# Cached pages on 16 partitions with eight rows each, in place of 32 partitions with four rows

## The chip, the cores and the metric

The kernel runs on one core of a Trainium2 chip. The metric is the device time of one execution, in microseconds; lower is better. Everything is float32.

## The reference, cut to what matters

One inference step of a two-layer decoder, for a prompt of 512 tokens and for 8 sequences of 8 new tokens each, which share all weights. Layer 0 has attention (differential attention over a paged cache, and a dilated window attention), layer 1 a convolution, and each layer ends in a mixture of 32 experts. The change lies in layer 0, in the attention of the 8 sequences over their cached pages:

```python
k_all = concatenate([cache_k_diff[i][page_table].reshape(n_dec, past, H_DIFF, 2 * HEAD_DIM), kd_new], axis=1)
v_all = concatenate([cache_v_diff[i][page_table].reshape(n_dec, past, H_DIFF, DV_DIFF), va], axis=1)
oa = diff_core(q1, q2, k_all[..., :HEAD_DIM], k_all[..., HEAD_DIM:], v_all, lam, pos_s, k_pos_s)
```

Each sequence has 2,048 cached positions in 16 pages of 128 rows. A row is 512 floats (2 KB), so a page is 256 KB, and a sequence's page keys and page values are 4 MB each. All new tokens may see all cached positions, so in which order the cached positions lie on the chip is free, as long as keys and values have the same one. Beside the pages each sequence has a window cache, of which 1,280 rows of keys and as many of values are read (2.5 MB each).

## The kernel before, in words

**Stages.** The projections of layer 0 run until about 200 us from the span's start. From 200 to 540 us comes the attention: the 64 items of the prompt (`prompt_*`) are interleaved with the 8 sequences b = 0 to 7. The output projection, the experts of layer 0 (both from 541 to 1,130 us), layer 1 and its experts follow; the change touches none of them.

**Buffers.** `Kd` and `Vd` hold the page keys and page values of one sequence, [128 partitions, 16, 512]; `Wkv` holds the window's keys, and after them the window's values. None of them is doubled: the next sequence's data can come only when the products of the last one have read the buffer.

**Loads.** `pages_in` (L553) issues one DMA for each page. Page j goes to partitions j % 4, j % 4 + 4, and so on, which is 32 partitions, and on each of them to four neighbouring places of the middle axis, with 8 KB in one piece. `window_far` (L559, three DMAs) and `window_near` (L564, one) load the window over all 128 partitions. The keys are issued by SyncE (SP), the values by GpSimd (POOL). An engine issues in the order of its code, so the order for sequence b is:

```python
sp.wait_ge(sd_mm, b)
pages_in(sp, pages[0:8], 0, ck, Kd, kd_in)
sp.wait_ge(pv_w, b)
window_far(sp, b, wk, kw_in)
window_near(sp, b, wk, kw_in)
pages_in(sp, pages[8:], 8, ck, Kd, kd_in)
```

POOL does the same with the values (L2553 to L2562): it waits for `pv_d` (the page value products of b - 1 are done), issues pages 0 to 7, waits for `sw_mm` (the window scores of b are done), issues the window and then pages 8 to 15. Below, K-first and K-second are the first and last eight pages of keys, V-first and V-second those of values.

**Use.** VectorE turns the page keys in place in 32x32 blocks, four of the 16 places at a time: `turn_pages(b, k)` (L1278) waits for the semaphore `kd_in[k]`, which the pages 4k to 4k + 3 raise. In the loop of VectorE (from L1498) the order is: k = 2 and 3 of sequence b after the window's maximum, and at the end of the round k = 0 and 1 of sequence b + 1 and then the two turns of its window keys. TensorE then computes the window scores (`window_scores`, L2048, semaphore `sw_mm`), the page scores (`page_scores`, L2063, `sd_mm`; they need all four turns), the window value products (`window_products`, L2110, `pv_w`, needs the window values), and the page value products (`page_products`, L2128, `pv_d`, needs all 16 pages of values). A round, here, is the time from the end of one sequence's page scores to the end of the next one's.

`page_numbers` (L548) reads the page table. `load_x` (L2508) is used below as a measure: after the attention it reads the prompt rows of x into 128 partitions and then the 64 sample rows into partitions 0 to 63.

Of the kernel before, what the change touches and what calls it, by code (L numbers as in the profile page):

```python
# [126 lines left out]
def build(nc, x_prompt, x_sample, ck, cv, wk, wv, st_rows, st_cols, ptab, w_in, w_out, w_pw1, w_pw2,  # L127
# [9 lines left out]
    def sem(name):  # L137
        return ctx.enter_context(nc.semaphore(name))
# [152 lines left out]
    kd_in, vd_in = [sem(f"kd_in{i}") for i in range(4)], [sem("vd_in")] * 4  # L291
# [13 lines left out]
    X_TILE = [16, 48, 16, 16, 16]  # L305
# [246 lines left out]
    def pages_in(eng, pages, first, src, dst, arrived):  # L552

        for j, page in enumerate(pages, first):
            held = dst[j % 4::4, j // 4 * 4:j // 4 * 4 + 4, :].rearrange("p n c -> p (n c)")
            rows_of = src[bass.ds(page, 1)].rearrange("a (p e) c -> (a p) (e c)", e=4)
            eng.dma_start(held, rows_of).then_inc(arrived[j // 4], 16)  # L557

    def window_far(eng, b, src, arrived):  # L559
# [16 lines left out]
    def _(sp):  # L576
# [36 lines left out]
        for i in range(4, 8):  # L613
            copy_window(i)
        sp.wait_ge(z_mm, Z_MM[1, "p4_1"])
        pages_in(sp, pages, 0, ck, Kd, kd_in)
        for b in range(1, NB):
            pages = page_numbers(sp, b)
# [6 lines that stand above are left out]
# [577 lines left out]
    def _(dve):  # L1202
# [75 lines left out]
        def turn_pages(b, k):  # L1278
            if not 0 <= b < NB:
                return  # L1280
            keys = Kd[:, 4 * k:4 * k + 4, :].rearrange("p n c -> p (n c)")
            dve.wait_ge(kd_in[k], X_TILE[k] + 64 * (b + 1))
            V.transpose(keys, keys).then_inc(kd_turned, 1)  # L1283

        link(V.memset(B(12288, 1024), 0.0))
# [43 lines left out]
        for w in range(3):  # L1329
# [33 lines left out]
            if w == 2:  # L1363
                turn_pages(0, 0)
# [4 lines left out]
            if w == 2:  # L1369
                turn_pages(0, 1)  # L1370
# [4 lines left out]
            if w == 2:  # L1375
                turn_pages(0, 2)
# [1376 lines left out]
```

## Time and profile before

| What | Value |
|---|---|
| Median of 3 runs | 1948.61 us (1948.54 to 1952.93) |
| The profiled execution's own time | 1950.49 us |
| Its span | 1948.5 us |
| PE busy | 1624.7 us, 83% |
| DVE busy | 695.3 us, 36% |
| DMA, mean rate over the span | 338 GB/s |
| Attention stage, end of the first to end of the eighth page scores | 239 to 520 us |

The span is the time between the first and the last instruction of the one execution that was profiled. Its own time is 2 us more than the span, and 1.9 us above the median. "DMA share" is the mean busy share of the 16 DMA engines, "GB/s" what they moved; a share can read a few per cent above 1, since a packet is counted where it starts.

### The profile page before, as it was taken

The numbers are of one execution on the slowest core, as the hardware profiler recorded it, in microseconds if no ns is written. First come the engines' busy times: TensorE is split into PE (matmuls) and PEld (weight loads), VectorE is DVE, ScalarE is ACT, GpSimd is POOL, SyncE is SP. The second block draws the span as 40 slices with busy tenths as digits, with TensorE's granted clock in tenths as the row PEclk, the third lists the DMA queues.
The fourth block names the chain that finished last, engine by engine and source line by source line (L and its number), as shares of the span: only waits on it lengthen the run. The fifth ranks groups of instructions, "written<-read, shape, count | busy, mean of one in ns | idle before, by whom it ended". The sixth has DMA issues, their size and how long they took to land.

```text
span 1948.5 us, 32623 instructions
## 1 busy us (share of the span) xinstructions
PE 1624.7 (83%) x12772; PEld 773.9 (40%) x12772; DVE 695.3 (36%) x1351; ACT 331.3 (17%) x769; POOL 213.5 (11%) x356
## 2 busy tenths in 40 slices
PE   7999788888898888878877879998968877877784
PEld 3444355555545322222222347764532222323231
DVE  4446478866514300000000159984260000000005
ACT  3100254444302000000000020013120000000001
POOL 1000222322200100000000030000021000000000
PEclk9999799978898899998999989999979989999998
DMA  9995489988853899999999999923269999999995
GB/s 347 346 357 194 178 322 358 362 323 333 349 221 136 332 428 426 409 429 427 428 427 428 415 289 322 324 99 162 80 255 426 428 416 418 427 428 427 428 426 206
DMA packets 83829, 659.20 MB, mean 338 GB/s; under 512 B 15307, under 2 KB 15436, under 8 KB 45418
## 3 DMA queue, kind: packets, MB, share of 16 engines
q1 hardware_dynamic: 58906, 569.86, 73.6%
q0 software_dynamic: 24800, 87.65, 12.0%
q8 instruction: 82, 1.34, 0.3%
q14 instruction: 41, 0.34, 0.0%
HBM read 643.18 MB, written 96.53 MB: 380 GB/s over the span
## 4 chain that ended last, share of the span: by engine, by line
PE 51%; DMA 34%; DVE 8%; issue 3%; ACT 2%; SPq 1%; POOLq 0%; DVEq 0%; POOL 0%; ACTq 0%
DMA ring<-in 30%; PE ps L2294 14%; PE ps L2249 7%; PE ps L2457 6%; PE ps L1874 6%; PE ps L1838 4%; PE ps L2063 2%; DMA ring<-y_rows 2%; PE ps L2478 2%; DVE ring L1283 2%; PE ps L2048 1%; PE ps L2314 1%; PE ps L2003 1%; DMA out<-x 1%; DVE ring L1276 1%
## 5 line engine op out<-in xcount | busy, mean ns | idle before, releaser
L2294 PE MATMUL ps<-ring,big 128*32 128x512 f32 (+1 forms) x2688 | 468.6, 645 | 134.0 <-DMA ring<-in 128.1
L2294 PEld LDWEIGHTS ps<-ring,big 128*32 128x32 f32 (+1 forms) x2688 | 146.9, 130 | 451.2 <-issue 381.2
L1555 DVE TENSOR_TENSOR big<-big,ps 128x512 f32<-128x512 f32 x32 | 22.0, 687 | 822.5 <-PE ps L2294 777.4
L2314 PE MATMUL ps<-ring,big 128*32 128x512 f32 (+1 forms) x928 | 215.7, 606 | 20.2 <-ACT big L797 12.3
L797 ACT ACTIVATE big<-ps 128x512 f32<-128x512 f32 (+6 forms) x166 | 84.2, 516 | 819.4 <-PE ps L1838 517.4
L2249 PE MATMUL ps<-ring,big 128*128 128x512 f32 (+1 forms) x288 | 122.7, 608 | 5.7 <-ACT big L1191 4.8
L2457 PE MATMUL ps<-act_t,ring 128*128 128x288 f32 x512 | 124.4, 406 | 0.0
L2314 PE MATMUL ps<-act_t,big 128*32 128x512 f32 (+1 forms) x416 | 99.0, 594 | 15.5 <-ACT big L797 10.5
L2457 PEld LDWEIGHTS ps<-act_t,ring 128*128 128x128 f32 x512 | 97.2, 190 | 26.8
L1779 DVE SCALAR_TENSOR_TENSOR big<-big,par 128x512 f32<-128x512 f32 x240 | 103.8, 503 | 0.0
L1874 PE MATMUL ps<-ring,act_t 128*128 128x512 f32 x208 | 94.8, 604 | 6.1 <-DMA ring<-in 4.1
L2314 PEld LDWEIGHTS ps<-ring,big 128*32 128x32 f32 (+1 forms) x928 | 63.6, 125 | 89.0 <-issue 89.0
L2602 POOL COPY sti<-sti 128x1 int32 (+1 forms) x30 | 5.5, 182 | 759.4 <-ACT big L797 759.4
L1838 PE MATMUL ps<-cst,big 128*128 128x128 f32 (+2 forms) x472 | 69.5, 296 | 21.9 <-DMA big<-h_rows,sti 8.8
L557 POOL DMA_DIRECT2D ring<-in x128 | 66.5, 524 | 193.8 <-PE ps L2128 179.9
L1838 PEld LDWEIGHTS ps<-cst,big 128*128 128x128 f32 (+2 forms) x472 | 59.9, 192 | 55.3 <-issue 30.1
L2249 PEld LDWEIGHTS ps<-ring,big 128*128 128x128 f32 (+1 forms) x288 | 51.1, 188 | 71.3 <-issue 68.6
L1283 DVE STREAM_TRANSPOSE ring<-ring 128x2048 f32<-128x2048 f32 x32 | 72.3, 2290 | 0.6 <-DMA ring<-in 0.6
L1109 ACT ACTIVATE big<-ps 128x512 f32<-128x512 f32 x32 | 19.1, 597 | 300.8 <-PE ps L2294 286.4
L1838 PE MATMUL ps<-cst,x 128*128 128x128 f32 (+1 forms) x312 | 54.8, 290 | 14.1 <-ACT x L797 9.4
L1874 PEld LDWEIGHTS ps<-ring,act_t 128*128 128x128 f32 x208 | 38.8, 193 | 50.9 <-issue 44.3
L2314 PEld LDWEIGHTS ps<-act_t,big 128*32 128x32 f32 (+1 forms) x416 | 28.6, 118 | 74.2 <-issue 74.2
(322 smaller groups left out, 1771.2 us busy)
## 6 DMA issues: line engine op xcount, KB each, us to landing
ring<-in SPq DMA_DIRECT2D x180, 2048.0 KB, 18.5
out<-in SPq DMA_DIRECT2D x16, 4080.0 KB
ring<-in SPq DMA_DIRECT2D x128, 256.0 KB, 7.0
ring<-in POOLq DMA_DIRECT2D x128, 256.0 KB, 5.8
act_t<-in SPq DMA_DIRECT2D x16, 2048.0 KB
ring<-in SPq DMA_DIRECT2D x28, 1024.0 KB, 10.1
ring<-in SPq DMA_DIRECT2D x24, 512.0 KB, 6.2
ring<-in POOLq DMA_DIRECT2D x24, 512.0 KB, 4.9
```

Of the source, the lines that this page charges most:

```text
L557: eng.dma_start(held, rows_of).then_inc(arrived[j // 4], 16)
L797: return A_(o, i, ACT.Copy)
L1283: V.transpose(keys, keys).then_inc(kd_turned, 1)
L1779: S(V.scalar_tensor_tensor(o, i, wdw[:, ch, j:j + 1], o, ALU.mult, ALU.add))
L1838: return nc.tensor.transpose(o, i, ident[0:n, 0:n])
L1874: ins = mm(ps[:, bank, :], lhs[:, k, :], rhs[:, k, :], start=(k == 0), stop=(k == 3))
L2063: ins = mm(ps[32 * c:32 * c + 16, g, :].rearrange("p (n k) -> p n k", n=16), Qrep[p, d, 16 * c:16 * c + 16], Kd[p, :, c * P + 32 * d:c * P ...
L2249: ins = mm(ps[unit_rows(t, j), i % 4, :], lhs(k, t), slot(slots_[n], 8)[:, k, :], start=(k == 0), stop=(k == KC - 1))
L2294: ins = mm(ps[half, i, :], XgT[:, par_, k, half], slot(eslots(w)[i], 8)[:, k, :], start=(k == 0), stop=(k == KC - 1))
L2314: ins = mm(ps[half, 5 + h, :], hbT[:, k, half], down_weights(w, odd)[:, k, h * 512:(h + 1) * 512], start=(k == 0), stop=(k == 3))
L2457: ins = mm(ps[:, 4 * (ch % 2) + 2 * i + h, 0:HALF], slot(first + i, 8)[:, k, (ch % 4) * P:(ch % 4 + 1) * P], act_t[:, k, h * HALF:(h + 1) ...
L2478: ins = mm(ps[32 * a:32 * a + 32, 4 + g, :], diag[p, 32 * a + j, :], taken, start=(j == 0), stop=(j == CK))
```

## The change: what it does

Page j now goes to partitions j % 8, j % 8 + 8, and so on, which is 16 partitions, and on each to eight neighbouring places, with 16 KB in one piece. Pages 0 to 7 together fill places 0 to 7 of the middle axis on all 128 partitions, pages 8 to 15 places 8 to 15. A turn of four places now needs eight pages, so the waits ahead of the turns k = 0 and k = 2 are for both semaphores of their half, and the turns k = 1 and k = 3 have no wait of their own.

```diff
     def pages_in(eng, pages, first, src, dst, arrived):
 
         for j, page in enumerate(pages, first):
-            held = dst[j % 4::4, j // 4 * 4:j // 4 * 4 + 4, :].rearrange("p n c -> p (n c)")
-            rows_of = src[bass.ds(page, 1)].rearrange("a (p e) c -> (a p) (e c)", e=4)
+            held = dst[j % 8::8, j // 8 * 8:j // 8 * 8 + 8, :].rearrange("p n c -> p (n c)")
+            rows_of = src[bass.ds(page, 1)].rearrange("a (p e) c -> (a p) (e c)", e=8)
             eng.dma_start(held, rows_of).then_inc(arrived[j // 4], 16)
...
             keys = Kd[:, 4 * k:4 * k + 4, :].rearrange("p n c -> p (n c)")
-            dve.wait_ge(kd_in[k], X_TILE[k] + 64 * (b + 1))
+            if k % 2 == 0:
+                for i in (k, k + 1):
+                    dve.wait_ge(kd_in[i], X_TILE[i] + 64 * (b + 1))
             V.transpose(keys, keys).then_inc(kd_turned, 1)
```

No instruction is added, removed or moved on any engine; on each engine they stand in the same order as before. What differs is the shape of the 256 page DMAs (128 on SP, 128 on POOL) and the waits of the turns.

## Rows read from the trace of the kernel before

**Rows 1.** The page, part 2: 40 equal slices of 48.7 us.
```profile
PEclk9999799978898899998999989999979989999998
DMA  9995489988853899999999999923269999999995
GB/s 347 346 357 194 178 322 358 362 323 333 349 221 136 332 428 426 409 429 427 428 427 428 415 289 322 324 99 162 80 255 426 428 416 418 427 428 427 428 426 206
```
**Rows 2.** Windows, one for each round: busy us, TensorE clock, DMA share, GB/s.
```profile
239.00:278.00 39.00, 35.15 (x679) 22.36 (x665) 31.18 (x42) 19.57 (x56) 10.57 (x20) 1.00 0.90 335
278.00:321.00 43.00, 36.55 (x694) 23.18 (x694) 33.23 (x57) 19.20 (x58) 10.36 (x20) 0.96 0.85 318
321.00:358.00 37.00, 33.62 (x668) 21.86 (x669) 29.43 (x44) 19.18 (x58) 10.37 (x20) 1.00 0.96 362
358.00:398.00 40.00, 32.73 (x661) 20.19 (x659) 30.34 (x54) 17.51 (x57) 10.37 (x20) 1.00 0.96 367
398.00:442.00 44.00, 38.88 (x651) 24.34 (x652) 28.02 (x44) 17.76 (x58) 10.36 (x20) 0.77 0.83 314
442.00:481.00 39.00, 32.31 (x643) 19.27 (x642) 28.59 (x55) 16.26 (x57) 9.85 (x19) 0.87 0.87 330
481.00:520.00 39.00, 32.27 (x634) 19.10 (x633) 26.41 (x44) 16.63 (x60) 10.89 (x21) 0.82 0.95 374
```
**Rows 3.** The chain that ended last, 355 to 520 us: start, us, what.
```profile
353.33 4.48 PE ps L2063 x128
...
396.83 1.07 PE ps L2063 x15
...
405.06 3.78 PE ps L2110 x80
...
412.50 1.00 PE ps L2128 x32
...
417.86 1.00 PE ps L2128 x32
...
488.37 7.48 DMA ring<-in
```
**Rows 4.** Timeline of SP, the issues of the keys.
```profile
146.58 10.82 SPq L557 DMA_DIRECT2D ring<-in  x16
...
239.59 5.06 SPq L557 DMA_DIRECT2D ring<-in  x8
...
357.98 5.14 SPq L557 DMA_DIRECT2D ring<-in  x8
364.36 2.48 SPq L562 DMA_DIRECT2D ring<-in  x3
366.88 0.59 SPq L566 DMA_DIRECT2D ring<-in  x1
367.66 6.13 SPq L557 DMA_DIRECT2D ring<-in  x8
398.14 6.20 SPq L557 DMA_DIRECT2D ring<-in  x8
```
**Rows 5.** Timeline of POOL, the issues of the values.
```profile
377.42 4.55 POOL L557 DMA_DIRECT2D ring<-in  x8 [23.74 <-PE ps L2128]
384.55 1.60 POOL L562 DMA_DIRECT2D ring<-in  x3 [2.58 <-PE ps L2048]
386.11 0.58 POOL L566 DMA_DIRECT2D ring<-in  x1
386.62 2.75 POOL L557 DMA_DIRECT2D ring<-in  x5
389.71 1.67 POOL L557 DMA_DIRECT2D ring<-in  x3 [0.34 <-issue]
```
**Rows 6.** Timeline of DVE, the turns of keys (L1283 pages, L1276 window).
```profile
175.96 2.30 DVE L1283 STREAM_TRANSPOSE ring<-ring 128x2048 f32<-128x2048 f32 x1
...
386.07 4.50 DVE L1283 STREAM_TRANSPOSE ring<-ring 128x2048 f32<-128x2048 f32 x2
...
411.46 4.50 DVE L1283 STREAM_TRANSPOSE ring<-ring 128x2048 f32<-128x2048 f32 x2
416.14 5.57 DVE L1276 STREAM_TRANSPOSE ring<-ring 128x3072 f32<-128x3072 f32 x2 [0.18 <-DMA ring<-in]
```
**Rows 7.** Windows: us, TensorE clock, DMA share, GB/s.
```profile
350.00:358.00 8.00, 1.00 1.03 422
...
547.00:548.00 1.00, 1.00 1.03 422
549.00:549.50 0.50, 1.00 0.83 164
549.50:550.00 0.50, 1.00 0.49 115
```
**Rows 8.** DMA landings: all page loads of L557, then DMAs issued 541 to 552 us.
```profile
DMA to landing us min/median/max: 2.9/6.4/17.5
...
x<-in POOLq DMA_DIRECT2D x1, 2048.0 KB, 8.7
x<-in POOLq DMA_DIRECT2D x1, 256.0 KB, 9.2
```

## The prediction

> **What bounds the kernel now.** I read the slices of the page first [rows 1]. Slices 5 to 10 are the attention: DMA is at eight or nine tenths of its time there, yet it moves 322 to 362 GB/s, where the expert stages (slices 14 to 21, 30 to 38) move about 428. So the queues are nearly full, but not saturated. The windows by round say the same more finely [rows 2]: seven rounds in 281 us, 40.0 us each, with PE busy for 34.5 us of a round and DVE for 29.6. The chain of waits [rows 3] runs through the engines in these rounds; a DMA of any length (7.48 us) stands in it only once, in the last round. The kernel is thus bound in this stage by the engines' own order of work, with the DMAs close behind.
>
> How close, I work out for one round. The page scores of one sequence end at 353.33 + 4.48 = 357.81 us, those of the next at 396.83 + 1.07 = 397.90 [rows 3]. Four batches of eight pages (2.10 MB each) and two windows (2.62 MB each) move in a round, 13.6 MB. In 350 to 358 us, when the value window and V-second are in flight, the rate is 422 GB/s at a share of 1.03 [rows 7]. At that rate a page takes 0.62 us, a batch 5.0 and a window 6.2, and a round has 4 x 5.0 + 2 x 6.2 = 32.4 us of DMA work in 40.0. The slack is 7.6 us, no more.
>
> **The change part by part.** *Issues.* SP needs 5.14 to 6.20 us for eight page DMAs and POOL 4.55 us [rows 4, 5]. Their number stays. The bounds are nothing and half (if the time goes by the rows of the DMA); I take nothing, because POOL issues a window DMA in 1.60 / 3 = 0.53 us and a page DMA in 4.55 / 8 = 0.57 [rows 5], although the window's has many more rows.
>
> *The waits of the turns.* The turns k = 0 and k = 1 stand back to back (4.50 us for both) [rows 6], so it is the first that now waits for pages 4 to 7 as well, 2.3 us earlier than they were wanted. K-first is issued from 398.14 to 404.34 [rows 4] and turned from 411.46 [rows 6], 7.1 us after its last issue; a page lands in 6.4 us (median, 2.9 at best) [rows 8]. At the rate of before this wait costs 0 to 1 us and I take 0. K-second: issued by 373.79, turned at 386.07, hidden by 12 us [rows 4, 6].
>
> *The transfers.* Here the change is decided. The pieces are 16 KB in place of 8 KB, which can help a little: the expert loads move 428 GB/s against 422 [rows 1, 7], 1.4%, 0.07 us in a batch. But a page now reaches only 16 partitions. The trace has one load that reaches a part of the partitions: the sample rows of x, into partitions 0 to 63, behind the prompt rows of x into all 128. While the latter run, the rate is 422 GB/s at a share of 1.03, which is 410 per full share. In the half microsecond when little but the 64-partition load is left, it is 164 at 0.83, which is 198, and in the next 115 at 0.49, 235 [rows 7]. The engines are busy and move half. (The small load also lands last though it is an eighth of the other: 9.2 us against 8.7 [rows 8].) So there are ways into the on-chip memory which DMA engines have to share if a transfer leaves the other ways out; and 32 partitions in steps of four do not have this trouble, they run at 422 [rows 7]. Whether steps of eight have it, no row shows. The bounds: full rate, 5.0 us a batch (4.9 with the longer pieces), and half rate, 9.9 us a batch of 2.10 MB at 211 GB/s. I take the half rate, since the 64-partition load is the nearest row in kind: 16 partitions cannot reach more ways than there are partitions, and the 32 of before may have needed all of theirs.
>
> The Trainium skill states the map ("SBUF — State Buffer", the section on the DMA port swizzle): bits 2 to 4 and bit 6 of the partition number pick one of 16 ports, so four neighbours share a port with the four that lie 32 further. By that rule j % 4 + 4m reaches all 16 ports, and j % 8 + 8m, in which bit 2 is fixed, only 8; pages 0 to 3 of a batch all go to the same 8 and pages 4 to 7 to the other 8. The row of the 64-partition load agrees with its statement that 0 to 63 reach 8 ports. By it a batch takes 9.9 us, and the sum is the one below; without the fixed bit it would be 5.0 us and the sum zero.
>
> *What half rate does to a round.* The DMA work becomes 4 x 9.9 + 2 x 6.2 = 52.0 us, against a round of 40.0: the cover of 7.6 us is gone and the DMAs are the bound. Not all of it is serial. When a page of the one queue and a page of the other go to different halves, both run, and 9.9 us of work counts 5. Follow the values: V-first is issued at 377.42, the window at 384.55, V-second at 386.62 [rows 5]. With 2 us until data flow they alone take 26.0 us, until 405.4 at the earliest, and later by some 3 us for the K-second batch that is still under way (K window and K-second issued from 364.36 [rows 4]: 364.4 + 2 + 6.2 + 9.9 = 382.5). Before, they needed 16.2 us and were done before 398. Now V-second still runs for about 10 us when K-first of the next sequence is issued at 398.14. K-first then takes 9.9 us if the two always lie in different halves, 19.8 if they never do; between these ends I take 15.5. It lands at 398.1 + 2.2 + 15.5 = 415.8, where the turns stood ready at 411.46 [rows 6]: a wait of 4.3 us. Behind it on the same queue the window of the keys (6.2 us) is free to start only then: 422.0 + 0.5, where its turn, shifted by the 4.3, stood at 420.4: 2 more. V-second itself is late by little: its products start at 412.50 [rows 3] and it ends near 411 to 418; I put 1 to 2 us, of which 1 lies beside the other waits. And all of DVE's work behind the turns (window maxima, page maxima, softmax of the prompt items) and PE's scores shift with them, nothing covers it. That makes about 7.5 us. The clock adds some: where PE has paused, the granted clock falls to the lower level, and the round at 0.77 took 44 us against 37 to 40 for those at 1.00 [rows 2]. With one pause of 6 us in each round I put 1.5 us for it, since part of a slower PE is waited out beside the DMAs anyway. A round comes to 49 us (+9), between +7 (halves always apart: 40.0 + 7) and +12 (52.0, no overlap at all).
>
> *The sum.* The rounds are not alike. The first has an idle queue ahead (K-first at 239.59 [rows 4], its V-second issued long before): +1. Six rounds at +9: +54. After the last page scores the last V-second (issued by 513.6) ends near 525, where its products begin at about 528: +1 with the output weights that run beside it. The page keys of the first sequence are issued from 146.58, with 16 x 0.6 us more work, and turned from 175.96 on [rows 4, 6]: hidden. Nothing outside the stage changes. 1 + 54 + 1 = **+56 us**. Against the profiled execution, 1950.5 + 56 = 2006.5; it stood 1.9 us above the median, so by the median the result is 1948.6 + 56 = 2004.6, about **2005 us**, +2.9%.
>
> **The rivals.** *The halves get out of step.* Two engines that share a way need not both be on the same half: if one gets ahead by four pages, it writes the second half while the other writes the first, and both run at full rate. For it: the rounds of before reach 422 although nothing tells the engines to alternate [rows 7]. Against it: a lead of four pages is 64 KB, a whole batch must then wait for the laggard, and batches of eight end often. A batch would take 7.5 us, the round 4 x 7.5 + 12.4 = 42.4 us of work with gaps of 2 to 4: about +3 a round, 1948.6 + 20 = 1969 us.
>
> *The ways are runs of eight partitions.* Steps of eight then reach each of them, batches stay at 5.0 us, and only the wait of the pair is left, 0 to 1 us in 7 rounds: 1945 to 1952, no change. The rows don't exclude it; the 64-partition row fits it as well.
>
> *Coarser pieces pay.* The other side: half the pieces, and issues that get cheaper with them. SP's eight page DMAs would take 5.1 - 1.5 us, and K-second, the window and V would land 1 us earlier; where turns follow landings at once (the window's, 0.18 us of idle [rows 6], and the 7.48 us in the chain [rows 3]), a round gains up to 1 us. 1948.6 - 7 = 1941 us. It decides if the DMA, not the engines' order, sets the window's turn in most rounds; the chain shows it in one.
>
> *It goes worse.* If one shared way also holds up what stands behind it in both queues, windows too, the work is 60 us a round: +18, 2055 us.
>
> **How the numbers follow.** What a measurement of this kernel can tell from no change is about 0.3%, 6 us. Half rate as forecast (1985 to 2035) 0.65; out of step (1957 to 1985) 0.13; worse (above 2035) 0.07; no change 0.09; faster 0.06. Slower takes the first three, 0.85; same 0.09; faster 0.06. The range reaches from 1960, which takes in nearly all of the second case, to 2040: some 0.2 is left out.
>
> **What would show it.** In the profile after: page batches in flight alone at about 211 GB/s with the DMA share near 1 (step 1); rounds of 47 to 52 us, the DMA share above 0.95 in each (step 2); turns of L1283's line idle before them for a DMA, 3 to 8 us in six of seven rounds, and the window's 1 to 3 (step 3); the stages from the output projection on as before, only later. The forecast is wrong if batches run at 400 GB/s or more, or if the share is full at half the rate and the rounds are still 40 us.

## The result, and the profile after

The change makes the kernel slower: 2068.63 us median of 4 runs (2059.91 to 2081.10), against 1948.57 us, the median of 4 runs of the kernel before beside it. The ratio is 1.062, with a 95% interval of 1.058 to 1.066. The direction was forecast; the size was not: +120 us, where +56 was forecast and 2040 us was the upper end of the range. The profiled execution took 2081.1 us with a span of 2079.0, 12 us above the median, so the sums below are for that execution: 2079.0 - 1948.5 = +130.5 us.

The slices of the page after, as [rows 1] for before (a slice is now 52.0 us):

```profile
PEclk9999889876876979999999998999998999999897
DMA  9994799988996449999999999993228999999995
GB/s 352 340 358 145 195 246 254 253 229 218 251 230 202 183 184 404 426 429 410 427 427 428 428 424 298 325 332 126 85 109 345 428 427 413 427 429 427 427 426 214
```

In the attention (slices 5 to 11) the DMA engines are busy for eight or nine tenths of the time, as before, but they move 218 to 254 GB/s in place of 322 to 362. The expert stages are untouched at 428.

The windows by round, as [rows 2]; they begin and end where the page scores of a sequence end. The columns are length, busy time of PE, PEld, DVE, ACT and POOL, the clock, the DMA share and GB/s:

```profile
244.00:297.00 53.00, 39.17 (x693) 23.06 (x680) 32.13 (x43) 19.59 (x56) 9.95 (x20) 0.87 0.99 253
297.00:350.00 53.00, 39.30 (x685) 24.35 (x678) 32.82 (x54) 19.17 (x57) 9.92 (x20) 0.87 1.00 256
350.00:405.00 55.00, 38.40 (x677) 23.63 (x669) 30.05 (x43) 19.36 (x58) 9.92 (x20) 0.84 0.99 248
405.00:462.00 57.00, 39.96 (x663) 23.96 (x661) 30.84 (x54) 17.80 (x57) 9.92 (x20) 0.76 0.89 228
462.00:526.00 64.00, 42.70 (x656) 24.48 (x653) 28.51 (x44) 17.69 (x59) 9.92 (x20) 0.73 0.88 221
526.00:581.00 55.00, 35.01 (x641) 20.33 (x639) 28.71 (x54) 16.38 (x57) 7.99 (x16) 0.78 0.98 245
581.00:637.00 56.00, 34.60 (x644) 20.83 (x631) 26.23 (x43) 16.40 (x58) 11.86 (x24) 0.73 1.00 248
```

Seven rounds took 393.0 us, 56.1 each against 40.0. DVE has the same 30 us of work in a round, PE 38 for 34.5, part of that because its granted clock is lower (0.73 to 0.87 here; 0.77 to 1.00 in the seven rounds of [rows 2]).

The chain that ended last, in the same stage, as [rows 3]. Before, a DMA of any length stood in it once; now one stands in each of the seven rounds (the first and the last, 11.86 and 24.83 us, are left out here and end at a turn of the window keys):

```profile
314.19 24.94 DMA ring<-in
...
366.61 27.50 DMA ring<-in
...
422.68 27.41 DMA ring<-in
...
481.13 34.62 DMA ring<-in
...
542.73 26.64 DMA ring<-in
```

All five of these end where the turns k = 2 and 3 begin: the chain waits for K-second, the last load in the queue of the keys. One round of these turns (L1285 pages, L1276 window), with the idle time ahead of each in brackets:

```profile
368.64 4.50 DVE L1285 STREAM_TRANSPOSE ring<-ring 128x2048 f32<-128x2048 f32 x2 [7.39 <-DMA ring<-in]
373.88 3.38 DVE L1276 STREAM_TRANSPOSE ring<-ring 128x3072 f32<-128x3072 f32 x1 [0.74 <-DMA ring<-in]
379.91 2.31 DVE L1276 STREAM_TRANSPOSE ring<-ring 128x2048 f32<-128x2048 f32 x1 [2.65 <-DMA ring<-in]
394.21 4.50 DVE L1285 STREAM_TRANSPOSE ring<-ring 128x2048 f32<-128x2048 f32 x2 [5.26 <-DMA ring<-in]
```

Over all seven rounds K-first is waited for 49.1 us, the window keys 19.3 and K-second 27.2, which is 7.0, 2.8 and 3.9 us a round.

Who waits, in sum: the turns of the page keys (as [rows 6], where nothing or 0.18 us stood ahead of a turn) and the value products. From the costliest groups; the last columns are idle time and its releaser:

```profile
L1285 DVE STREAM_TRANSPOSE ring<-ring 128x2048 f32<-128x2048 f32 x32 | 72.3, 2292 | 76.3 <-DMA ring<-in 76.3
...
L2130 PE MATMUL ps<-ring,act_t 128*16 128x128 f32 x1024 | 46.6, 336 | 38.7 <-DMA ring<-in 35.6
```

The same turns cost the same 72.3 us as before; the 76.3 us of idle time before them was 0.6. The two longest rounds, the fourth and the fifth, are also those in which the DMA engines are not full (0.89 and 0.88). In the fourth, K-second lands at 450.09 us (422.68 + 27.41 in the chain), although the DMAs stand nearly still before that:

```profile
436.00:440.00 4.00, 0.90 0.17 47
```

A share of 0.17 is two to three engines of 16, and the packets that they move are those of the key queue. They are behind the others, and the wait is for them. Why they are behind was not looked into.

And windows in which little but page loads is in flight (as [rows 7]; in 355 to 360 us mostly K-first, in 442 to 449 V-first):

```profile
355.00:360.00 5.00, 4.78 (x101) 3.45 (x102) 3.04 (x8) 3.96 (x11) 0.00 (x0) 1.00 1.05 243
...
442.00:449.00 7.00, 5.75 (x168) 3.71 (x146) 5.37 (x15) 2.66 (x9) 5.18 (x11) 1.00 1.04 225
```

That is 231 and 216 GB/s per full share, where the loads of before gave 410 [rows 7], and the forecast took 211.

### The profile page after: what moved, and what is told of

It reads as the page before. It is cut to its first block, busy times and chain, and to the rows that moved or that the text cites. A ratio compares the mean times of both kernels' runs of the same rounds, so it can differ in the third digit from the quotient of the medians.

```text
span 2079.0 us, 32638 instructions
## 1 busy us (share of the span) xinstructions
PE 1666.6 (80%) x12772; PEld 790.6 (38%) x12772; DVE 698.3 (34%) x1351; ACT 332.3 (16%) x769; POOL 210.2 (10%) x356
## 4 chain that ended last, share of the span: by engine, by line
PE 45%; DMA 42%; DVE 5%; issue 3%; SPq 3%; ACT 1%; POOLq 1%; POOL 0%; DVEq 0%; ACTq 0%
DMA ring<-in 39%; PE ps L2296 13%; PE ps L2251 6%; PE ps L2459 6%; PE ps L1876 6%; PE ps L1840 3%; PE ps L2065 2%; DMA ring<-y_rows 2%; PE ps L2480 2%; PE ps L2316 1%; SPq L557 1%; DMA out<-x 1%; PE ps L2112 1%; PE ps L2335 1%; PE ps L2223 1%
## 5 line engine op out<-in xcount | busy, mean ns | idle before, releaser
L2316 PE MATMUL ps<-ring,big 128*32 128x512 f32 (+1 forms) x928 | 215.7, 606 | 17.8 <-ACT big L797 12.3
L1285 DVE STREAM_TRANSPOSE ring<-ring 128x2048 f32<-128x2048 f32 x32 | 72.3, 2292 | 76.3 <-DMA ring<-in 76.3
L2316 PEld LDWEIGHTS ps<-ring,big 128*32 128x32 f32 (+1 forms) x928 | 63.7, 125 | 86.5 <-issue 86.5
L557 POOL DMA_DIRECT2D ring<-in x128 | 62.4, 492 | 287.0 <-PE ps L2130 257.8
L2130 PE MATMUL ps<-ring,act_t 128*16 128x128 f32 x1024 | 46.6, 336 | 38.7 <-DMA ring<-in 35.6
L2065 PE MATMUL ps<-ring 32*16 32x512 f32 x1024 | 50.3, 801 | 29.2 <-DVE ring L1285 25.3
L1840 PE MATMUL ps<-cst,x 128*128 128x128 f32 (+1 forms) x312 | 54.9, 290 | 13.6 <-ACT x L797 9.2
```

Of the source, the lines that this page charges most:

```text
L1840: return nc.tensor.transpose(o, i, ident[0:n, 0:n])
L2065: ins = mm(ps[32 * c:32 * c + 16, g, :].rearrange("p (n k) -> p n k", n=16), Qrep[p, d, 16 * c:16 * c + 16], Kd[p, :, c * P + 32 * d:c * P ...
L2130: ins = mm(ps[32 * c:32 * c + 16, 7, P:2 * P], PT_d[:, n, 16 * c:16 * c + 16], Vd[:, n, c * P:(c + 1) * P], start=(n == 0), stop=False)
L2316: ins = mm(ps[half, 5 + h, :], hbT[:, k, half], down_weights(w, odd)[:, k, h * 512:(h + 1) * 512], start=(k == 0), stop=(k == 3))
```

## The experiments

The question was in two parts: is it the partitions that a page reaches, and why is the loss twice what that was priced at? For all kernels below I also give the window from the end of the first to the end of the eighth page scores. Its DMA share times the length of a round is what I call the **engine time** of a round: how long a DMA engine was held in it, in the mean of the 16. A **packet** is what one engine moves in one go, here one piece on one partition; the trace has the time that each took. In the expert loads a packet of 16 KB takes 0.61 us, and the shortest of 8 KB in the attention take 0.31. In the change those of the pages (16 KB) take 1.21 us in the median.

The rounds come from the one profiled execution of each kernel. Executions of one kernel differ by up to some 20 us, and in e11 by 43 us, so a difference of one or two us between rounds says little.

**e1: the waits alone.** The layout of before, with the pair waits of the change.

```diff
-            dve.wait_ge(kd_in[k], X_TILE[k] + 64 * (b + 1))
+            if k % 2 == 0:
+                for i in (k, k + 1):
+                    dve.wait_ge(kd_in[i], X_TILE[i] + 64 * (b + 1))
```

> The layout of before with the change's waits alone: the turns k = 0 and 2 wait for all eight pages of their half. Theory H (a page on partitions in steps of eight has only half of the ways into the on-chip memory): the waits are nearly free, 0 to 1 us a round, ratio to before 1.000 to 1.003. Theory W (the wait for twice the pages is what holds VectorE and all behind it): most of the +120 us stays, ratio above 1.03.

Measured: ratio 1.002 (1.000 to 1.004), rounds of 39.8 us. The waits are free, as forecast; theory W falls.

**e2: 32 partitions, but half of the ways.** Everything as before but the choice of the 32 partitions.

```diff
-            held = dst[j % 4::4, j // 4 * 4:j // 4 * 4 + 4, :].rearrange("p n c -> p (n c)")
+            lo = j % 2 + 64 * (j % 4 // 2)
+            held = dst[lo:lo + 63:2, j // 4 * 4:j // 4 * 4 + 4, :].rearrange("p n c -> p (n c)")
```

> Pages on 32 partitions with 8 KB pieces and the waits of before, but in steps of two, inside partitions 0 to 63 (pages 0, 1 of each four) or 64 to 127 (pages 2, 3). Number of partitions, size and number of pieces and the waits are all as before; only which partitions is changed. Theory H: page batches at about half rate again, the 8 KB packets take about twice their 309 ns, rounds of 50 to 57 us, ratio 1.04 to 1.07. Theory L (fewer, longer pieces or fewer partitions are what is slow): as before, ratio 1.00, rounds of 40 us.

Measured: 1.051 (1.047 to 1.055), rounds of 54.0 us. The number of partitions, of pieces, the size of a piece and the waits are those of before, and most of the change's loss is there. The 8 KB packets (a fifth of them the window's) take 0.57 us in the median, where those of before take 0.31. The rows are read from the same places in the same order as before, so it is not the source either. Theory L falls for that part.

**e3: the change in pieces of 8 KB.**

```diff
-            held = dst[j % 8::8, j // 8 * 8:j // 8 * 8 + 8, :].rearrange("p n c -> p (n c)")
-            rows_of = src[bass.ds(page, 1)].rearrange("a (p e) c -> (a p) (e c)", e=8)
+            held = dst[j % 8::8].rearrange("p (h q r) c -> p q h (r c)", h=2, q=2)[:, j // 8]
+            rows_of = src[bass.ds(page, 1)].rearrange("a (p h e) c -> (a p) h (e c)", h=2, e=4)
...
-            keys = Kd[:, 4 * k:4 * k + 4, :].rearrange("p n c -> p (n c)")
+            g = (0, 2, 1, 3)[k]
+            keys = Kd[:, 4 * g:4 * g + 4, :].rearrange("p n c -> p (n c)")
```

> The change's 16 partitions in steps of eight, but each partition's eight rows in two pieces of 8 KB that lie 16 KB apart on chip (places 0 to 3 and 8 to 11, or 4 to 7 and 12 to 15). Theory H: no better than the change, ratio 1.05 to 1.07. Theory L in the form that the 16 KB piece is slow: back to before, ratio 1.00 to 1.01.

Measured: 1.055 (1.052 to 1.058), rounds of 54.9 us, 0.60 us for a packet of 8 KB. The length of the piece is not what is slow.

**e4: neighbours in the queue in different halves.** The change, with a batch issued in another order.

```diff
-        for j, page in enumerate(pages, first):
+        for j, page in sorted(enumerate(pages, first), key=lambda jp: (jp[0] % 4, jp[0])):
```

> The change, but each batch issues its pages in the order 0, 4, 1, 5, 2, 6, 3, 7, so that neighbours in a queue go to different halves of the ways. Theory H with engines that keep in step: two engines that share a way still meet on it, ratio 1.05 to 1.07. Theory H with engines that get one page out of step (as seems to happen over 8 KB pieces before): batches near 5 to 7 us in place of 9, ratio 1.00 to 1.03. Theory L: no effect, ratio 1.06.

Measured: 1.040 (1.035 to 1.045), rounds of 50.1 us. The same bytes on the same partitions, and a third of the loss is gone: it matters which pages are in flight together. A packet takes 1.07 us, still far from 0.61: the order gives back some of the time, and not the full rate that the theory with a ratio of 1.00 to 1.03 needs.

**e5 and e6: keys alone, values alone.** `pages_in` takes w = 8 or 4 by the semaphores it is given; e5 has the pair waits too.

```diff
-            held = dst[j % 4::4, j // 4 * 4:j // 4 * 4 + 4, :].rearrange("p n c -> p (n c)")
-            rows_of = src[bass.ds(page, 1)].rearrange("a (p e) c -> (a p) (e c)", e=4)
+            w = 8 if arrived is kd_in else 4
+            held = dst[j % w::w, j // w * w:j // w * w + w, :].rearrange("p n c -> p (n c)")
+            rows_of = src[bass.ds(page, 1)].rearrange("a (p e) c -> (a p) (e c)", e=w)
```

> Only the page keys lie on 16 partitions in steps of eight (with the change's waits), the values on 32 in steps of four as before; the positions of keys and values then differ, so the attention over the pages is not the reference's. Theory S (slack: a round of 40.0 us has 32.4 us of DMA work, each half-rate batch adds 4.9 us, and only what goes past the round costs): 42.2 us of work, rounds of 41 to 44, ratio 1.01 to 1.02. Theory A (each slow batch costs its own length, however much slack there is): half of the change's loss, ratio 1.03.

> Only the page values lie on 16 partitions in steps of eight, the keys as before with the waits of before; the attention over the pages is not the reference's. Theory S: 42.2 us of work, ratio 1.01 to 1.02, and less than with the keys, since the values are needed later after their issue (21 us against 7). Theory A: ratio 1.03, and keys and values alone add up to the change's 1.06.

Measured: keys 1.032 (1.030 to 1.035), rounds of 48.7 us; values 1.027 (1.023 to 1.031), rounds of 46.7. Theory S as I had put it falls: there was hardly any slack in front of the first slow batches. The sum, 0.059, is nearly the change's 0.062, which is the number of theory A; whether A's reason holds was left to e9, e10 and e12.

**e7: the other queue begins with the other half.**

```diff
-        for j, page in enumerate(pages, first):
+        jobs = list(enumerate(pages, first))
+        if arrived is vd_in and len(jobs) == 8:
+            jobs = jobs[4:] + jobs[:4]
+        for j, page in jobs:
```

> The change, but POOL issues each batch of values with the second four pages first, so that its batches start in the other half than the batches of keys. Theory O (batches of keys and values in flight together both run at full rate if they are in different halves): the K-first and V-second that meet get faster, rounds of 47 to 50, ratio 1.03 to 1.045. Theory N (an engine has one piece of work at a time, and the engines that share a way have the same one, so it makes no difference what order the other queue has): ratio 1.055 to 1.07, as the change.

Measured: 1.062 (1.060 to 1.065), rounds of 55.7 us, as the change. Theory O falls, and with it a step of the prediction.

But the edit does the reverse of what its name says. From the place of a packet in its batch (the first 64 of 128 are pages 0 to 3 of it) one can tell its half. In the change, packets of both queues that were in flight together, where that can be told, already lay in different halves in 672 of 871 cases; in e7 they lay in the same half in 707 of 900. The traces settle the question both ways: in different halves a packet of the change took 1.17 us, in the same half one of e7 took 1.25, and neither is near 0.61. In this stretch of the change, K-second's last pages and V-first's first ones are in flight, in different halves, at 217 GB/s for a full share:

```profile
378.00:382.00 4.00, 1.00 1.00 217
```

**e8: 64 partitions in steps of two.** The same lines with 2 for 4: `dst[j % 2::2, j // 2 * 2:j // 2 * 2 + 2, :]`, e=2.

> Pages on 64 partitions in steps of two with two rows each (4 KB pieces), waits of before (the turn k waits for its own four pages; each now fills two places of all partitions by pairs). All 16 ways are reached. Theory H: full rate but for the shorter pieces (159 ns for 4 KB against 309 for 8 KB, 3%), DMA work 32.9 us a round, ratio 0.998 to 1.005. Theory that fewer partitions are better where the ways are all reached and more are worse: ratio above 1.01.

Measured: 1.001 (0.9995 to 1.002), rounds of 39.5 us. More partitions and shorter pieces cost nothing as long as all ways are reached.

**e11: 16 neighbouring partitions.** The change, with a page in a run.

```diff
-            held = dst[j % 8::8, j // 8 * 8:j // 8 * 8 + 8, :].rearrange("p n c -> p (n c)")
+            lo = 16 * (j % 8)
+            held = dst[lo:lo + 16, j // 8 * 8:j // 8 * 8 + 8, :].rearrange("p n c -> p (n c)")
```

> The change's 16 partitions with one piece of 16 KB each and its waits, but page j on the 16 neighbouring partitions from 16 (j % 8). Theory H with the port map as the Trainium skill (SBUF — State Buffer, port swizzle) states it: such a run reaches 4 of 16 ports. As a mechanism of this kernel: four engines share a way, a 16 KB packet takes about 4 x 611 = 2440 ns, 32 pages in a round are 78 us of engine time and the windows 12 to 16 more, rounds of 90 to 95 us, ratio 1.18 to 1.22. Theory H2 (a page on 16 partitions, or in one piece for each engine, gets half, whichever the partitions are): as the change, packets of 1170 ns, ratio 1.06.

Measured: 1.112 (1.104 to 1.120), rounds of 71.7 us (in a profiled execution of 2189.25 us; the four lie from 2152.71 to 2195.88): neither of the two. H2 is excluded, the same 16 partitions in number and the same 16 KB pieces cost nearly twice as much in another place. Theory H has the direction, but a packet takes 1.60 us in the median, not its 2.44. Two windows of e11 (length, clock, DMA share, GB/s):

```profile
415.00:430.00 15.00, 0.66 0.91 148
443.00:453.00 10.00, 0.67 1.06 127
```

That is 163 and 120 GB/s per full share: a quarter of 410 is 103, a half 205, and neither window comes down to the quarter. Each page here takes another set of ways than the one before it, so engines that are a page apart do not meet; this is my reading, as for e4, and was not shown by itself.

**e9 and e10: less to load before the change.** `part` is true for the sequences 1 to 7, in e9 for the values, in e10 for both.

```diff
+            if part:
+                held, rows_of = held[:, 0:1024], rows_of[:, 0:1024]
             eng.dma_start(held, rows_of).then_inc(arrived[j // 4], 16)
```

> The kernel before, with only the first 4 KB of each 8 KB piece of the page values loaded for the sequences 1 to 7 (the rest keeps the last sequence's), so the attention over the pages is not the reference's; all waits and instructions stay. DMA engine time in a round falls by 32 x (309 - 159) ns = 4.8 us, from 36.0 to 31.2. Theory E (before the change the engines' order sets the round, and the DMAs are covered with some us to spare): rounds stay at 38.5 to 40, ratio 0.995 to 1.00. Theory D (the round is the DMA engine time and about 4 us, before the change too): rounds of 35 us, 1915 us, ratio 0.98 to 0.985.

> The same for keys and values: DMA engine time in a round 26.4 us; the attention over the pages is not the reference's. Theory E: rounds of 38 to 40 us, ratio 0.99 to 1.00. Theory D: rounds near 31 us, 1885 us, ratio 0.965 to 0.97; or, where the engines' order is met on the way, a stop between 34 and 37.

Measured: both 0.998 (0.9965 to 0.9994, and 0.9963 to 0.9997), rounds of 40.0 and 38.8 us. Theory E holds: with a quarter less engine time (table below) the round of before is nearly the same, the order of the engines sets it. (The profiled execution of e9 was the slowest of its ten and that of e10 the fastest, so the 1.2 us between their rounds are within what executions differ by.)

**e12: less to load after the change.** The same with `[:, 0:2048]` of 4096, for keys and values.

> The change, with only the first 8 KB of each 16 KB piece of page keys and page values loaded for the sequences 1 to 7, so the attention over the pages is not the reference's; partitions, waits and the number of transfers are the change's. Theory M (a round is the longer of two: 39 to 40 us by the engines' order, or the DMA engine time and 1 to 3 us): at half rate a piece of 8 KB takes about 600 ns, the engine time of a round is 53.8 - 32 x 0.57 = 35.6 us, rounds of 39 to 41 us, ratio 0.998 to 1.01. Theory A (each transfer on half of the ways delays by its own length): the loss is halved with the bytes, ratio 1.03.

Measured: 1.009 (1.005 to 1.013), rounds of 41.2 us. The value lies where theory M put it, and A's 1.03 is excluded: a slowed transfer costs almost nothing if the round has room for it. The engine time came out at 31.7 us, not 35.6, since the 8 KB pieces did better than half rate (the packets of this size spread from 0.31 to 0.65 us). What is left, 0.9% of the time and 1.2 us of the round, is not explained by engine time.

Below is one window of each kernel, from the first to the eighth page scores. The second number is its length, which is seven rounds; the last two are DMA share and GB/s.

Before:

```profile
239.40:519.40 280.00, 240.59 (x4609) 149.90 (x4609) 206.70 (x334) 125.84 (x401) 72.77 (x140) 0.91 0.90 342
```

After:

```profile
244.30:637.30 393.00, 269.14 (x4608) 160.62 (x4609) 209.29 (x334) 126.39 (x401) 69.49 (x140) 0.80 0.96 242
```

E1, the waits alone:

```profile
237.00:515.80 278.80, 239.42 (x4608) 147.95 (x4609) 206.87 (x334) 125.60 (x401) 72.89 (x140) 0.92 0.91 345
```

E2, 32 partitions of one half:

```profile
237.80:615.90 378.10, 271.72 (x4608) 161.09 (x4609) 209.88 (x334) 126.20 (x401) 71.51 (x140) 0.78 0.98 250
```

E3, pieces of 8 KB:

```profile
240.50:625.10 384.60, 281.28 (x4608) 166.92 (x4609) 208.89 (x335) 126.33 (x401) 70.73 (x140) 0.77 0.98 246
```

E4, alternating order:

```profile
241.70:592.70 351.00, 260.95 (x4608) 156.08 (x4609) 208.80 (x334) 126.11 (x401) 69.45 (x140) 0.82 0.99 272
```

E5, keys alone:

```profile
241.80:582.80 341.00, 266.94 (x4611) 160.22 (x4609) 208.93 (x334) 125.95 (x401) 72.60 (x140) 0.80 0.94 282
```

E6, values alone:

```profile
240.80:567.40 326.60, 259.61 (x4608) 159.31 (x4609) 207.68 (x334) 126.25 (x401) 69.80 (x140) 0.84 0.96 291
```

E7, opposite halves:

```profile
243.00:632.60 389.60, 279.29 (x4611) 166.25 (x4609) 208.50 (x334) 126.30 (x401) 69.39 (x140) 0.77 0.97 243
```

E8, 64 partitions:

```profile
236.10:512.70 276.60, 234.79 (x4609) 145.83 (x4609) 206.76 (x334) 125.83 (x401) 73.90 (x140) 0.94 0.93 346
```

E9, values halved:

```profile
240.10:520.00 279.90, 240.75 (x4608) 147.94 (x4609) 206.95 (x334) 126.03 (x401) 73.05 (x140) 0.92 0.80 291
```

E10, keys and values halved:

```profile
237.20:508.80 271.60, 235.51 (x4608) 146.71 (x4609) 206.73 (x334) 125.70 (x401) 73.19 (x140) 0.93 0.71 246
```

E11, runs of 16:

```profile
250.40:752.20 501.80, 296.35 (x4610) 174.66 (x4609) 209.10 (x334) 126.71 (x401) 69.76 (x140) 0.71 0.97 190
```

E12, the change halved:

```profile
241.20:529.70 288.50, 242.66 (x4608) 148.67 (x4609) 207.53 (x334) 125.97 (x401) 69.75 (x140) 0.91 0.77 232
```

Worked out from these rows, by engine time:

| Kernel | Engine time of a round, us | Round, us | Ratio |
|---|---|---|---|
| e10, keys and values halved | 27.5 | 38.8 | 0.998 |
| e12, the change halved | 31.7 | 41.2 | 1.009 |
| e9, values halved | 32.0 | 40.0 | 0.998 |
| before | 36.0 | 40.0 | 1 |
| e1, waits | 36.2 | 39.8 | 1.002 |
| e8, 64 partitions | 36.7 | 39.5 | 1.001 |
| e6, values alone | 44.8 | 46.7 | 1.027 |
| e5, keys alone | 45.8 | 48.7 | 1.032 |
| e4, alternating | 49.6 | 50.1 | 1.040 |
| e2, half the ways on 32 | 52.9 | 54.0 | 1.051 |
| e3, 8 KB pieces | 53.8 | 54.9 | 1.055 |
| after | 53.9 | 56.1 | 1.062 |
| e7, opposite halves | 54.0 | 55.7 | 1.062 |
| e11, runs of 16 | 69.5 | 71.7 | 1.112 |

The table is the result of the study. Up to about 37 us of engine time a round takes 39 to 41 us. From 45 us on it takes the engine time and 0.5 to 3 us. The change moves the kernel from the one branch to the other. Both columns come from the same trace, so the table tells what bounds a round, and does not forecast the engine time of a layout that has not run; and it is a mean of seven rounds, of which the fourth and fifth of the change took 6 and 8 us more than their engine time.

## Why the prediction was right and wrong

**Direction, and what is slow: right.** Page batches run at about half rate per held engine (231 and 216 GB/s against 410), because of which partitions a page reaches. e2 shows it with all else as before, e3 excludes the length of the pieces, e8 shows that more partitions and shorter pieces cost nothing by themselves, and e11 gives a third place with a third price. By the map of the Trainium skill ("SBUF — State Buffer", the DMA port swizzle) a page reaches 16 ports before and in e8, 8 in the change, e2 and e3, and 4 in e11. The order of the prices agrees with it, the height of the last does not (163 to 120 GB/s per full share, not 103). The rival that the ways are runs of eight partitions, the one that coarser pieces pay and the one that the engines get out of step within a batch have fallen. The size was right within a little: the page packets hold an engine for 37.2 us of a round, 9.3 a batch, where 9.9 was forecast.

**Issues and the pair waits: right.** Priced at nothing; e1 measures 1.002, and POOL's eight page issues take 4.51 us after against 4.55 [rows 5].

**"The slack is 7.6 us, no more": wrong, the term was mis-sized.** I had divided bytes by the best rate, 422 GB/s, and got 32.4 us of DMA work in a round. But the engines are held longer than that, and the share of the seven rounds said so, of which [rows 2] has the parts: 0.90 x 40.0 = 36.0 us. The 8 KB packets of before take 0.33 us in the mean, where the shortest take 0.31; why was not looked into. The slack was 4.0 us. With it, keys alone come to 36.0 + 9.8 = 45.8 us, which is the engine time of e5; values alone measured 44.8.

**"9.9 us of work counts 5" where keys and values lie in different halves: wrong, this overlap does not exist.** It was the step that took the round from +12 down to +7.5. The pages of the two queues did lie in different halves for most of the time that they were in flight together, and still took 1.17 us a packet in place of 0.61; where e7 puts them into the same half for most of it, the kernel takes the same time. Without this overlap, and from the right base, the forecast's own working gives 36.0 + 4 x 4.9 = 55.6 us a round. Measured are 53.9 of engine time and 56.1 for the round: +16.1, where +9 was forecast and +12 was my upper bound. Seven rounds are +113 of the +130.5 us. The lower bound does not follow from the working either: with the halves always apart, K-first would have landed at 410.2, ahead of its turns at 411.46, and not 7 us late.

Why there is no such overlap was not settled. A slow page holds its engine, and the engine serves both queues; that would fit the packets, but no run takes it apart. e4 shows that pages of one queue can gain from another order.

My 1.5 us for the clock were not tested; 2.2 us a round are left above the engine time, and in two rounds the engines were not full, so there is room for it.

**"K-second: hidden by 12 us": wrong, this wait was put at nothing.** The forecast had 4.3 us at K-first and 2 at the window. Measured are 7.0, 2.8 and, at K-second, 3.9 us, together 13.7 of the 16.1 us that a round got longer; K-second stands in the chain in five of seven rounds. The 12 us of cover were those of before; by the forecast's own times the batch would have ended at 382.5, 3.6 us ahead of its turns, with V-first already on the same engines from 377.42.

**"The first has an idle queue ahead: +1": wrong.** The first round took 53.3 us (244.29 to 297.61), where it had taken 41.0 (239.41 to 280.40): +12.3. Its four batches are as slow as all others, and the DMAs are full through it (share 0.99).

**The start and the end: wrong.** I had +2 us. The first page scores end 4.9 us later. Of that 3.9 us are in one piece of the chain, after the projections (first of before, then of after):

```profile
206.02 5.87 POOLq L348
```

```profile
207.83 9.78 POOLq L348
```

L348 is the drain in the fence between the stages, and just before it POOL issues V-first of the first sequence. It got longer by 3.9 us, and so did the slowest landing of that batch (4.2 us from issue before, 8.1 after). At the end, from the eighth page scores to the output projection, 32.6 us pass in place of 21.5: +11.1. The chain shows the last V-second behind it, which I had put at "+1":

```profile
627.64 28.31 DMA ring<-in
656.09 1.91 PE ps L2130 x32
```

It was issued from 623.7 us, behind V-first (612.9) and the window (621.6), with K-second of this sequence, waited for until 626.66, still under way; I had let it have the engines almost alone. The output weights, issued at 637.3, share the engines with it. The rest of the kernel is 1.5 us longer: 4.9 + 113 + 11.1 + 1.5 = 130.5.

**The rival "it goes worse"** came nearest in time (2055 us), but its mechanism, windows held up as well, is not what happened in the main: the window's 8 KB packets take 0.31 us in the median of the change too. Its 60 us a round is also more than the 53.9 measured.

**What bounds before: right, and narrow.** The reading that the engines' order sets the round of 40 us and the DMAs are close behind is what e9 and e10 show.

**The signs named beforehand.** Batches near 211 GB/s came (231 and 216). Rounds of 47 to 52 us did not (52.5 to 63.7), nor a share above 0.95 in each (0.89 and 0.88 in two). The turns of L1285 waited 7 to 17 us in six of seven rounds, where 3 to 8 was named.

## What to carry to other kernels

Add up DMA work by how long the engines are held (share times time), and not by bytes over the best rate: the difference was 3.6 of a supposed 7.6 us of cover here. In this kernel a round followed this sum once it passed what the compute engines need, and below that a quarter less bought 0.2%. Follow also the last load of each queue, not only the one that arrives next: here the longest waits in the chain were for K-second, which had been hidden by 12 us. When a tile is laid over a part of the partitions, what counts is which ones: steps of two (64 partitions) and four (32) were equal here, steps of eight (16) and steps of two within one half of the partitions cost 5 to 6% of the whole kernel, for the same bytes.

## What was not expected of the hardware

Loads of two queues do not speed each other up when their pages lie in different halves (1.17 us a packet, 0.61 at full rate; e7 with the same half, 1.25 us and 1.062 for the whole kernel, as the change), while a change of order within both queues gives back a third of the loss (e4: 1.040, 1.07 us a packet). Pages on 16 neighbouring partitions (e11) gave 163 GB/s per full share in one stretch and 120 in a later one. Two or three of 16 engines can be well behind the rest, and the wait is for them (share 0.17 in 436 to 440 us, K-second landed at 450.09). And the drain of POOL took 5.87 us before and 9.78 after the change, right behind a batch of loads that it had issued itself, whose slowest landing grew by the same 3.9 us: it seems to last until those have landed, which a fence after a prefetch would then have to pay. No run moves the batch away from the fence to show it.
